# A norm's scaling moved from GpSimd to TensorE, and the gate pieces of the attentions gathered in every second step

## What is computed

```python
# layers 1 and 2: eight heads of 64 columns that share keys (a), four heads of 128 columns in two halves (b)
mix = sigmoid(gate_a) * (o_a @ w_branch_a) + sigmoid(gate_b) * (o_b @ w_branch_b)
return mix @ w_out
# layer 3: eight heads of 64 columns (c), then
mixed = (gate_a * (y_attn @ w_branch_attn) + gate_b * (y_rwkv @ w_branch_rwkv)) @ w_out
x = layer_norm(ALPHA * x + mixed, ln_g[0], ln_b[0])     # y = (x - mu) * rsqrt(var + eps) * g + b
moe = hier_moe(x, router_grp, ..., exp_gate, exp_up, exp_down)   # 2 of 32 experts per token
```

## Time and profile before

| | us |
|---|---|
| median of three runs (2903.09 to 2918.70) | 2905.33 |
| the profiled execution, its time | 2917.54 |
| the profiled execution, its span | 2915.9 |
| PE busy | 2667.5 (91%) |
| DVE busy | 1658.9 (57%) |
| ACT busy | 1186.5 (41%) |
| POOL busy | 143.8 (5%) |
| granted TensorE clock, mean (1.00 is 2.4 GHz, 0.5 is 1.2 GHz) | 0.946 |

### The profile page before, as it was taken

One profiled execution on the slowest core, in us unless ns is written; L12 is line 12 of the kernel. 1 busy time (PEld: TensorE's weight loads), 2 busy tenths in 40 slices (PEclk: granted clock), 3 DMA queues, 4 the chain that ended last, 5 costly groups with the idle time before them and its releaser, 6 DMA issues.

```text
span 2915.9 us, 36619 instructions
## 1 busy us (share of the span) xinstructions
PE 2667.5 (91%) x14888; PEld 2027.4 (70%) x14888; DVE 1658.9 (57%) x2735; ACT 1186.5 (41%) x1806; POOL 143.8 (5%) x109
## 2 busy tenths in 40 slices
PE   6998999999998998999999999899999999779876
PEld 5776777888876776768788887576766667644435
DVE  4497555646456378645655455535445525588767
ACT  3214653424234222653433243336223323368765
POOL 0010000000000010000000000000000000223210
PEclk9899999999999899999999999799989999889998
DMA  3121232222221121223222222222100124579982
GB/s 120 58 73 65 84 119 87 101 90 98 101 87 62 58 73 52 84 97 116 94 88 101 95 83 98 101 75 78 59 26 29 66 75 167 224 275 395 403 350 100
DMA packets 64285, 336.01 MB, mean 115 GB/s; under 512 B 9584, under 2 KB 10352, under 8 KB 31088
## 3 DMA queue, kind: packets, MB, share of 16 engines
q1 hardware_dynamic: 58992, 325.19, 31.0%
q0 software_dynamic: 5120, 8.40, 0.9%
HBM read 313.63 MB, written 28.31 MB: 117 GB/s over the span
## 4 chain that ended last, share of the span: by engine, by line
PE 82%; DVE 11%; ACT 3%; issue 3%; DMA 1%; SPq 0%; POOL 0%; POOLq 0%; DVEq 0%; ACTq 0%
PE bank L899 15%; PE bank L901 15%; PE bank L900 15%; PE bank L1087 4%; PE bank L1089 3%; PE bank L1088 3%; PE bank L3130 2%; PE bank L3131 2%; PE bank L3146 2%; PE bank L2287 2%; PE bank L1131 2%; DVE wl L1335 1%; PE bank L1159 1%; PE bank L1151 1%; DVE arena L1504 1%
## 5 line engine op out<-in xcount | busy, mean ns | idle before, releaser
L899 PE MATMUL bank<-XH,wh 128*128 128x512 f32 x1312 | 529.6, 404 | 15.0 <-DVE XL L1376 10.9
L900 PE MATMUL bank<-XL,wh 128*128 128x512 f32 x1312 | 518.7, 395 | 0.0
L901 PE MATMUL bank<-XH,wl 128*128 128x512 f32 x1312 | 518.2, 395 | 0.0
L1335 DVE TENSOR_TENSOR wl<-raw,wh 128x2048 fp32r<-128x2048 f32 (+1 forms) x165 | 364.8, 2212 | 153.6 <-ACT wh L1863 153.5
L1863 ACT ACTIVATE wh<-raw 128x2048 fp32r<-128x2048 f32 (+1 forms) x165 | 303.3, 1840 | 180.8 <-DMA raw<-in_W 180.7
L899 PEld LDWEIGHTS bank<-XH,wh 128*128 128x128 f32 x1312 | 250.9, 191 | 92.8 <-issue 20.0
L901 PEld LDWEIGHTS bank<-XH,wl 128*128 128x128 f32 x1312 | 251.0, 191 | 53.8
L900 PEld LDWEIGHTS bank<-XL,wh 128*128 128x128 f32 x1312 | 251.5, 192 | 52.0 <-issue 2.4
L899 PE MATMUL bank<-arena_rounded,wh 128*128 128x512 f32 x576 | 232.0, 403 | 5.3 <-DVE arena_rounded L1580 3.2
L901 PE MATMUL bank<-arena_rounded,wl 128*128 128x512 f32 x576 | 230.3, 400 | 0.0
L900 PE MATMUL bank<-arena_rounded,wh 128*128 128x512 f32 x576 | 230.2, 400 | 0.0
(11 more groups left out here) (539 smaller groups left out, 4580.4 us busy)
## 6 DMA issues: line engine op xcount, KB each, us to landing
raw<-in_W SPq DMA_DIRECT2D x153, 1024.0 KB, 4.9
arena<-in_WE SPq DMA_DIRECT2D x32, 1024.0 KB, 23.5
raw<-in_WE SPq DMA_DIRECT2D x21, 1024.0 KB, 24.1
wh_full<-in_WE SPq DMA_DIRECT2D x21, 1024.0 KB, 24.7
hT<-in_WE SPq DMA_DIRECT2D x14, 1024.0 KB, 25.9
gsave<-scr SPq DMA_DIRECT2D x48, 256.0 KB, 3.9
scr<-gsave SPq DMA_DIRECT2D x48, 256.0 KB, 4.0
cst<-in_WE SPq DMA_DIRECT2D x8, 1024.0 KB, 24.4
```

Source lines behind the costliest of these rows:

```text
L899: pe.matmul(ps[0:c.stop - c.start, :], h[:, k, c], hi, start=i == 0, stop=False)
L900: pe.matmul(ps[0:c.stop - c.start, :], h[:, k, c], lo, start=False, stop=False)
L901: mm = pe.matmul(ps[0:c.stop - c.start, :], l[:, k, c], hi, start=False, stop=i == len(xs) - 1)
L1335: w_lo.inc(dve.tensor_tensor(wl[:, i % 3, 0:k], raw[:, i % 3, 0:k], wh[:, i % 3, 0:k].bitcast(F32), ALU.subtract), i)
```

## The change

It has two parts. In the attentions the pieces of an odd step move to the even step ahead of it wherever heads have 64 columns; steps of kind b keep four each. In the norm POOL's two passes per token tile go away: PE multiplies the transposed blocks again by diagonals of the gain (`gained`), adds mean times gain and root times bias as a product over two rows (`offset`), and ACT's copy out of the bank scales by the reciprocal root (`normal`). For that the mean and the root of each token are transposed into two rows (`flat`). The order of the embeds, transposes, squares and copies is rearranged, the memset of POOL comes earlier, and only one row of gain and one of bias are loaded instead of 128 copies of both.

```diff
         def fill(m, s):
             if m == 2:
-                return 2 if s < 8 else 1 if s < 32 else 0
-            return 4 if s < 16 else 2 if s < 48 else 0
+                return 0 if s % 2 or s >= 32 else 4 if s < 8 else 2
+            return 4 if s < 16 or s % 2 == 0 and s < 48 else 0
...
-            for half in range(2):
-                for ti in range(4):
-                    bank.plan(("token", half, ti), 4 + ti)
+            for name in ("token", "gained"):
+                for half in range(2):
+                    for ti in range(4):
+                        bank.plan((name, half, ti), 4 + ti)
+            bank.plan(("flat", 0), 3)
...
-            rows_in.inc(sync.dma_start(flat(scr[:, 0:4, :]), A["rows"][0]), 7)
+            for q in range(2):
+                rows_in.inc(sync.dma_start(GB7[q:q + 1, :], A["rows"][0, 0:1, 1024 * q:1024 * q + 1024]), (7, q))
...
-                if i:
-                    to_tokens(i - 1)
+                for k in ((), (0,), (1,), (2,), (3,), (), (4, 5), (6,))[i]:
+                    to_tokens(k)
             to_tokens(7)
 
         def tensor_router(pe, opened, embed_some):
-            for i in range(8):
+            def gained(half, ti):
+                ps = opened(("gained", half, ti))
+                for c in range(4):
+                    k = 4 * half + c
+                    pe.matmul(ps[:, tt(c)], hT[:, k, tt(ti)], DIAG[:, k, :], start=c == 0, stop=False, skip_group_check=True)
+
+            def offset(half, ti):
+                key = ("gained", half, ti)
+                mm = pe.matmul(bank.ap(key), FLAT[:, tt(ti)], GB7[:, 512 * half:512 * half + 512], start=False, stop=True,
+                               skip_group_check=True)
+                bank.filled(mm, key)
+
+            pe.wait_ge(*lnv("diag"))
+            for i in range(3):
+                embed_some(i)
+            for ti in range(4):
+                gained(0, ti)
+            ps = opened(("flat", 0))
+            pe.wait_ge(*lnv("mean"))
+            pe.wait_ge(*lna("root"))
+            for ti in range(4):
+                mm = pe.matmul(ps[64:66, tt(ti)], MSD[:, ti, :], ident, start=True, stop=True)
+            bank.filled(mm, ("flat", 0))
+            pe.wait_ge(*rows_in((7, 1)))
+            pe.wait_ge(*bank.empty(("flat", 0)))
+            for ti in range(4):
+                offset(0, ti)
+            for i in range(3, 6):
+                embed_some(i)
+            for ti in range(4):
+                gained(1, ti)
+                offset(1, ti)
+            for i in range(6, 8):
                 embed_some(i)
...
@@ scalar_tokens @@
-                ins = act.activation(PP2[:, ti, :], xn[:, ti, 0:512], ACT.Square, bias=NM0[:, ti:ti + 1], accum_out=M0[:, ti:ti + 1])
+                ins = act.activation(xn[:, ti, 512:1024], bank.ap(key), ACT.Square, bias=NM0[:, ti:ti + 1],
+                                     accum_out=M0[:, ti:ti + 1])
...
-            for ti in range(4):
-                key = ("token", 1, ti)
-                col = slice(ti, ti + 1)
-                bank.emptied(act.activation(xn[:, ti, 512:1024], bank.ap(key), ACT.Identity, scale=RSTD[:, col],
-                                            bias=NMR[:, col]), key)
-                lna.inc(act.activation(xn[:, ti, 0:512], xn[:, ti, 0:512], ACT.Identity, scale=RSTD[:, col],
-                                       bias=NMR[:, col]), ("z", ti))
...
@@ scalar_router @@
-            for i in range(4):
+            for i in range(3):
+                embedded(i)
+            act.wait_ge(*bank.full(("flat", 0)))
+            bank.emptied(act.activation(FLAT, bank.ap(("flat", 0))[64:66, :], ACT.Copy), ("flat", 0))
+            act.wait_ge(*lnv("rec"))
+            for ti in range(4):
+                normal(0, ti)
+            for i in range(3, 6):
                 embedded(i)
             act.wait_ge(*routed("gd"))
             exped.inc(act.activation(gd, gd, ACT.Exp), "gd")
-            for i in range(4, 8):
+            for ti in range(4):
+                normal(1, ti)
+            act.wait_ge(*bank.full(("embed", 2, 7)))
+            for i in range(6, 8):
                 embedded(i)
...
@@ vector_tokens @@
             for k in range(8):
+                if k == 5:
+                    dve.wait_ge(*lna("sum0"))
+                    lnv.inc(dve.tensor_scalar(NM0, NM0, -1.0 / 512, None, ALU.mult), "mean0")
...
-                if k == 6:
-                    dve.wait_ge(*lna("sum0"))
-                    lnv.inc(dve.tensor_scalar(NM0, NM0, -1.0 / 512, None, ALU.mult), "mean0")
+                if k == 5:
+                    for q in range(2):
+                        dve.wait_ge(*p_lo((2, q)))
+                    for q in range(8):
+                        ins = dve.tensor_scalar(DIAG[:, q, :], ident, K("lng", q), None, ALU.mult)
+                    lnv.inc(ins, "diag")
...
@@ pool_router @@
-            for ti in range(4):
-                pool.wait_ge(*lna(("z", ti)))
-                g.inc(pool.tensor_tensor(xn[:, ti, :], xn[:, ti, :], LN_G7, ALU.mult))
-                offset(ti)
-            pool.wait_ge(*xnorm(3))
-            pool.wait_ge(*bank.full(("embed", 2, 7)))
+            pool.wait_ge(*x((("mix", 2), 7)))
             pool.memset(scr[0:SLOT, 0:6, :], 0.0).then_inc(zeroed, 1)
...
@@ sync_router @@
-                sync.wait_ge(*xnorm(ti))
+                sync.wait_ge(*bank.empty(("gained", 1, ti)))
                 sync.dma_start(xtok[128 * ti:128 * ti + 128, :], xn[:, ti, :]).then_inc(tok_out, 16)
```

More of the change, by code:

```diff
@@ L631, in program @@
         tok_out = sem("tok_out")
-        lnv = Signal(sem("lnv"), ["wx", "mean0", "mean1", "var", "rec"])
-        lna = Signal(sem("lna"), ["sum0", "sq0", "sq1", "root"] + [("z", ti) for ti in range(4)])
-        xnorm = Signal(sem("xnorm"), range(4))
+        lnv = Signal(sem("lnv"), ["wx", "mean0", "diag", "mean1", "mean", "var", "rec"])
+        lna = Signal(sem("lna"), ["sum0", "root"])
         routed = Signal(sem("routed"), ["gd", "dd", "oab", "extra", "own", "owner", "onehot", "slots"])
@@ L685, in program @@
         PP2 = scr[:, 7:15, :]
[L686 removed]
+        PH2, PL2 = R3(12288, 2), scrr[:, 13:15, :]
         uh, ul = R3(0, 8), R3(4096, 8)
@@ L2906, in scalar_tokens @@
                 act.wait_ge(*bank.full(key))
[L2907 to L2918 removed]
+                if ti == 0:
+                    for t_ in range(4):
+                        act.wait_ge(*bank.empty(("token", 0, t_)))
+                ins = act.activation(xn[:, ti, 512:1024], bank.ap(key), ACT.Square, bias=NM1[:, ti:ti + 1],
+                                     accum_out=M1[:, ti:ti + 1])
+                bank.emptied(ins, key)
+            act.wait_ge(*lnv("var"))
+            lna.inc(act.activation(SD, RSTD, ACT.Sqrt), "root")
         def scalar_router(act):
@@ L2923, in embedded, with normal @@
                 bank.emptied(act.activation(PP2[:, i, :], bank.ap(("embed", 2, i)), ACT.Copy), ("embed", 2, i))
-            for i in range(4):
+            def normal(half, ti):
+                key = ("gained", half, ti)
+                act.wait_ge(*bank.full(key))
+                bank.emptied(act.activation(xn[:, ti, 512 * half:512 * half + 512], bank.ap(key), ACT.Copy,
+                                            scale=RSTD[:, ti:ti + 1]), key)
+            for i in range(3):
[6 more added lines that the diff above has]
+            for i in range(3, 6):
                 embedded(i)
@@ L2981, in vector_tokens @@
             bank.emptied(ins, key)
-            dve.wait_ge(*lna("sq1"))
+            for ti in range(4):
+                dve.wait_ge(*bank.empty(("token", 1, ti)))
             vv(dve.tensor_tensor(M1, M0, M1, ALU.add))
```

31 lines of the change are left out of this document (13 added, 18 removed).

## The result

| | before | after |
|---|---|---|
| median (four executions each), us | 2912.01 | 2971.72 |
| the profiled execution, its time | 2917.54 | 2967.65 |
| its span | 2915.9 | 2966.1 |
| granted clock, mean | 0.946 | 0.940 |

The ratio of the times is 1.020 (95% interval 1.016 to 1.024): slower by some 60 us on the medians, by 50.2 in the spans of the two profiled executions. The forecast was slower by 22.6: its sign was right, its size was not, and 2971.7 lies above the range. So I work in stages of the two traces: an attention stage goes from its first 64-column scores to the first product behind it.

What follows compares the result with a forecast made beforehand. PE was taken as the bound, carrying 82% of the chain, so waits between its work matter. Two layers +20, third attention +5, norm -2.4 make +22.6 on the median 2905.3: 2928 us, range 2896 to 2944.

Steps and rivals of the forecast that it cites:

- (a) to (e): 64-column attention steps, per layer: group starts -1.3, step waits +10.0, column sums +2.8, covered waits -2.5, step 48 +1.3; +10.3.
- the group starts: Attention, part of (a) to (e): one matmul group less per pair of steps saves 16 x 0.08, -1.3 us a layer.
- rival (1): Attention: ACT's and DVE's copies come in time, a layer -3.8, the third -1.3; total 2894 us; chance 0.20.
- rival (3): Attention stages: PE's clock falls on the new waits, +12 to +20 us, 2942 taken; chance 0.13.
- Norm, what PE gets: Norm: embeds, diagonals, two-row products and mean/root transposes queue on PE ahead of the rank matmuls, from 2516.0 to 2542.8.
- the term of -2.4: Norm stage's net: rank matmuls run about twice as fast behind work, 2.1 us for 4.4; bounds -9 to +4.
- The "wrong" sign named for it: Norm: rank matmuls waiting for oab would show the forecast wrong and rival (2) right.
- rival (2): Norm: with POOL gone, DVE's chain gains 15.7 us in full; total 2915 us; chance 0.12.
- DVE's lock: Norm's router: POOL's passes stretch DVE's chain from 5 to 21 us; without them every DVE row 0.3 or less.
- nothing, up to 3 if late: Token stores on SP behind weight blocks awaiting embed 7: 4 MB land by about 2554, before the gather at 2561.
- faster by more: Chance 0.12 that the kernel is faster by more than 14.5 us: rival (2) with rival (1), and half of rival (1).

Runs made afterwards that it cites:

- j: Kernel before with attention pieces gathered, weight splits at the early steps of the new count, gate copies and low-rank tiles at the old steps; ratio 1.010.
- c: Kernel before with attention pieces gathered as in the change, but splits, gate copies and low-rank tiles kept at their old steps; ratio 1.001.
- l: Kernel before with only the gathered attention pieces, plus unread filler products on PE ahead of its waits in steps 28, 36, 44 of two layers; 2956.22 us, ratio 1.0134.
- b: Changed kernel with the attention's gathering of pieces taken back, so only the new norm; 2924.26 us, ratio 1.0038.
- g: Kernel before with GpSimd's eight norm passes over the tokens replaced by one-element memsets; 2902.81 us, ratio 0.9960.
- e: b with rank, count, basis and owner matmuls moved ahead of the last five embeds and second half of the diagonals; ratio 1.0010.
- h: b with the eight two-row products run over 128 rows, of which 126 are zero; ratio 0.9967.

## Why the prediction was wrong

Point by point, by its own steps.

- **(a) to (e), the waits:** right in sum. Idle time of PE grew by 10.4 in layer 1 and 10.8 in layer 2 (forecast 11.6 without the group starts), by 4.7 in the third attention (forecast 6.3; its terms add up to 5.6, not to the 5 taken). L1155 waited longest 2.0, L1163 1.6, the column sums L942 2.7 (forecast 2.8). The early splits are the cause (j against c). The gain named for copies that come in time, -3.8 a layer in rival (1), is not there: c, whose splits and copies stand at the old steps, is at +0.8, with 1.2 us of wait at the column sums and a clock of 0.98. So rival (1) is refuted in its place and in its price.
- **The clock, rival (3): the step that failed.** I had the waits right, priced a clock that falls on them at 12 to 20 us, and then kept it out of the sum as a case of its own with a chance of 0.13. It belonged in the sum. The busy time of the same matmuls grew by 9.4, 5.9 and 3.3 us, 18.5 together, on top of 3.9 that the group starts should have saved. This lies in the 12 to 20 of rival (3); its time of up to 2948 still falls short, by what the norm cost. The row that misled me was the one I leaned on: 5.5 us of idle time at 1.00. It is made of waits of 1.2 at the longest and of one of 1.61 that ends the stage, and right behind that one, outside the window, the clock of the kernel before had fallen: its products take 0.63 us there, where those of the earlier trace rows take 0.40.

```profile
399.40 0.73 PE L899 MATMUL bank<-arena_rounded,wh 128*128 128x512 f32 x1 [1.61 <-DVE arena_rounded L1580]
399.92 0.63 PE L900 MATMUL bank<-arena_rounded,wh 128*128 128x512 f32 x1
```

  The fourth row, too, had shown 0.94 with 2.9 us idle in 30. What l shows is that filled waits keep the clock; what it does not show, and what stays open, is why the same pair of waits takes it down in one place and not in another. The Trainium skill, TensorE: Matmul & The Clock Gate, section HAM oscillation, tells of a kernel that waits some 3 to 5 us for a DMA between its groups of matmuls and whose clock is throttled again every time. The traces differ from it in two ways: the clock fell behind waits of 1.6 to 2.7 us, and behind the pairs eight times in twelve.
- **Norm, what PE gets:** one price was too low and the clock again missing. Forecast for the stretch: 26.8 us from the last transposes; with full rows and the clock at 1.00 it is 27.2. With two rows it is 33.7 (b) and 38.1 (the changed kernel). A block of diagonals with its two-row product takes 2.14 at full clock where 1.7 were forecast (0.8 and 0.9), 1.8 us for four blocks; the rest, some 5 us in b and 9.5 in the changed kernel, is clock, by estimate. So the term of -2.4 measured +9.2, and +4.4 in b: here the sign was wrong too. The "wrong" sign named for it, rank matmuls that wait for `oab`, did not come, and rival (2) is refuted: DVE gave its time back and PE had no use for it.
- **DVE's lock:** right. Every single DVE instruction of the router is at 0.3 or less, `oab` 27 us early. From L3011 to `oab` the chain takes 6.0 us in g and 21.9 before (5 and 21 in the forecast, which counts eleven stretched instructions where ten with two inputs stand there).
- **SP and the gather:** I had "nothing, up to 3 if late". In the changed kernel it was hidden by PE. In e, where PE reached the place products earlier, the gather waited for the stores.
- **The base:** the median of before rose from 2905.3 (three executions) to 2912.0 (four) and to 2911 to 2914.6 beside the experiments. That is some 7 us of the distance between 2928 and 2971.7, and no step of mine.
- **Two small sums:** the bounds of the norm's term, added up from their own parts, are about -9.6 and +2.8, not -9 and +4; and the chance of "faster by more" is 0.04 + 0.10 = 0.14, not 0.12. Neither moves the range.

The sum by stages: forecast 20 + 5 - 2.4 = 22.6; measured 19.8 + 16.7 + 8.0 + 9.2 = 53.7, of which 18 to 22 are clock in the attentions (22 if the group starts saved what was forecast, which no run shows apart). Of the stretch to the rank, 10.9 us in the changed kernel (6.5 in b) come, against h, from the two-row products, 1.6 of the 6.5 as their price at full clock.

## What to carry to other kernels

A wait on the engine whose clock is gated can cost twice: once for itself, and again for the work after it that runs at half speed (here behind eight pairs of twelve), so such waits belong into the sum with their clock, priced from rows at either level, and not beside it as a rival. When events hang on a count (splits, copies), moving the counted work moves the events; fix them apart, and test which of the two costs. And when a chain is freed, look for the next queue in line before believing the gain: here PE's order, and behind it the stores of the tokens.

## What the hardware showed that I had not expected

PE's clock fell while PE was busy. In the stretch of b that holds eight float products with two rows of data it was 0.85 with 0.8 us of idle time; the same columns over 128 rows, of which 126 are zero, left it at 1.00. A stretch almost without idle time is no promise of the clock. Between diagonals the 512-column product was also slower with two rows than with 128 at full clock, 1.05 us against 0.86, and so were the diagonals beside it, 1.09 against 0.89. Both went with the number of rows alone: the two that carry data lie at partitions 64 and 65 in either kernel. Why is not shown.

The same code fell further in one execution than in another (0.74 and 0.85 in the norm), and in one of two like layers further than in the other (0.90 and 0.94). That stays open.
